# Stick-breaking exponents: a sum of the softplus of later key blocks, and one product with it per key block

## The reference, cut to what matters

```
z = q k^T * scale                                   # 512 queries x 512 keys, per head
causal = key < query
log_keep = where(causal, log_sigmoid(-z), 0)
suffix = reverse_cumsum_over_keys(log_keep) - log_keep
attn = where(causal, exp(log_sigmoid(z) + suffix), 0)
out = attn v
```

## Time and profile before

| | |
|---|---|
| median of 3 runs | 2204.77 us (2204.25 to 2207.14) |
| the profiled execution | 2204.68 us, its span 2202.9 us |
| PE busy | 2169.7 us, 98% of the span |
| DVE busy | 1253.3 us, 57% |
| ACT busy | 773.4 us, 35% |
| POOL busy | 25.7 us, 1% |
| HBM | 212.06 MB read, 98 GB/s over the span |

### The profile page before, as it was taken

One profiled execution on the slowest core, in us unless ns is written; L12 is line 12 of the kernel. 1 busy time (PEld: TensorE's weight loads), 2 busy tenths in 40 slices (PEclk: granted clock), 3 DMA queues, 4 the chain that ended last, 5 costly groups with the idle time before them and its releaser, 6 DMA issues.

```text
span 2202.9 us, 25712 instructions
## 1 busy us (share of the span) xinstructions
PE 2169.7 (98%) x10775; PEld 1804.6 (82%) x10775; DVE 1253.3 (57%) x1611; ACT 773.4 (35%) x1022; POOL 25.7 (1%) x42
## 2 busy tenths in 40 slices
PE   6999999999999899999999999999999999999998
PEld 3888888888888788987888888889898788888887
DVE  5898797953663847433855554234743475555422
ACT  2323232223353245344343333135434434333321
POOL 1000000000000000000000000000000000000000
PEclk9999999999999999999999999999999999999999
DMA  8432322333223122322223222322232222222322
GB/s 294 141 105 90 115 82 96 100 111 99 95 90 125 60 96 77 116 77 73 87 73 113 96 96 96 105 67 96 77 116 77 77 96 77 96 96 97 106 94 77
DMA packets 184151, 217.92 MB, mean 99 GB/s; under 512 B 3804, under 2 KB 159076, under 8 KB 184036
## 3 DMA queue, kind: packets, MB, share of 16 engines
q1 hardware_dynamic: 180048, 210.52, 28.8%
q10 hardware_dynamic: 3252, 3.60, 0.5%
q0 software_dynamic: 736, 2.15, 0.3%
HBM read 212.06 MB, written 4.19 MB: 98 GB/s over the span
## 4 chain that ended last, share of the span: by engine, by line
PE 94%; DVE 3%; ACT 1%; issue 1%; DMA 1%; POOL 0%; SPq 0%; POOLq 0%; ACTq 0%; DVEq 0%
PE psum L1640 30%; PE psum L1641 29%; PE psum L1642 29%; PE psum L1914 1%; PE psum L1945 1%; PE psum L1748 1%; PE psum L1977 1%; PE psum L1957 1%; DVE whl L475 1%; DMA ada<-in_w_ada 1%; DVE hT L1342 0%; PE psum L1901 0%; PE psum L1930 0%; POOL stat L620 0%; ACT hT L808 0%
## 5 line engine op out<-in xcount | busy, mean ns | idle before, releaser
L1640 PE MATMUL psum<-hT,whl 128*128 128x512 f32 (+1 forms) x2112 | 802.7, 380 | 7.7 <-DVE hT L1342 5.5
L1642 PE MATMUL psum<-hT,whl 128*128 128x512 f32 (+1 forms) x2112 | 795.9, 377 | 0.0
L1641 PE MATMUL psum<-hT,whl 128*128 128x512 f32 (+1 forms) x2112 | 795.9, 377 | 0.0
L475 DVE TENSOR_TENSOR whl<-raw,whl 128x1024 fp32r<-128x1024 f32 (+1 forms) x368 | 446.9, 1216 | 456.4 <-ACT whl L468 456.3
L468 ACT ACTIVATE whl<-raw 128x1024 fp32r<-128x1024 f32 (+1 forms) x368 | 384.2, 1047 | 445.6 <-PE psum L1642 430.8
L1640 PEld LDWEIGHTS psum<-hT,whl 128*128 128x128 f32 x2112 | 398.4, 189 | 89.0 <-issue 11.3
L1642 PEld LDWEIGHTS psum<-hT,whl 128*128 128x128 f32 x2112 | 398.3, 189 | 73.0
L1641 PEld LDWEIGHTS psum<-hT,whl 128*128 128x128 f32 x2112 | 398.6, 189 | 71.5 <-issue 0.5
L1640 PE MATMUL psum<-whl,ff 128*128 128x512 f32 x352 | 137.1, 389 | 0.0
L1642 PE MATMUL psum<-whl,ff 128*128 128x512 f32 x352 | 136.9, 389 | 0.0
L1641 PE MATMUL psum<-whl,ff 128*128 128x512 f32 x352 | 136.9, 389 | 0.0
(11 more groups left out here) (278 smaller groups left out, 2146.2 us busy)
## 6 DMA issues: line engine op xcount, KB each, us to landing
raw<-in_w_in SPq DMA_DIRECT2D x88, 1024.0 KB, 5.1
raw<-in_w_up SPq DMA_DIRECT2D x44, 1024.0 KB, 5.1
raw<-in_w_down SPq DMA_DIRECT2D x20, 1024.0 KB, 5.0
ada<-in_w_ada SPq DMA_DIRECT2D x12, 1024.0 KB, 14.3
raw<-in_w_branch SPq DMA_DIRECT2D x12, 1024.0 KB, 5.1
raw<-in_w_out SPq DMA_DIRECT2D x12, 1024.0 KB, 5.1
x<-in_x SPq DMA_DIRECT2D x4, 512.0 KB, 7.3
v_by_token<-vnat ACTq DMA_DIRECT2D x4, 512.0 KB, 2.9
```

What stands on the lines that cost most here:

```text
L475: nc.vector.tensor_tensor(whl_view(w, 1), raw_view(w), whl_view(w, 0).bitcast(F), ALU.subtract).then_inc(w_lo, 1)
L1640: M(out_, stat_hi, mov_hi, start=start, stop=False, **kw)
L1641: M(out_, stat_hi, mov_lo, start=False, stop=False, **kw)
L1642: return M(out_, stat_lo, mov_hi, start=False, stop=stop, **kw)
```

## The change

The softplus of the later key blocks is summed on DVE. `sbt` (640 columns) holds, for key block 0, the sum of the blocks 1 to 3 (384 columns), and for key block 1 the sum of the blocks 2 and 3 (256 columns); for key block 2 the only later block is block 3 itself. ACT makes the fp32r part of `sbt` and DVE its low part, and PE multiplies `negones_r` with these once per key block and part. That leaves (2+2) + (2+2) + (2+2) + 2 = 14 fp32r matmuls and 4 bfloat16 ones per head. The buffers lie in the memory of `sba`, the exponentials of the same pair, which ACT writes later; so DVE waits, for heads 2 and 3, until PE has read `sba` of the pair before (`sbo_ps`).

```diff
+    sbt = [over(f"sbt{e}", (sb_at[e] + 10) * K + 2560, [P, 640]) for e in range(2)]
+    sbt_hi = [over(f"sbt_hi{e}", (sb_at[e] + 10) * K, [P, 640], R) for e in range(2)]
+    sbt_lo = [over(f"sbt_lo{e}", (sb_at[e] + 10) * K + 2560, [P, 640], R) for e in range(2)]
...
                 def sb_hi(h):
                     act.wait_ge(sp_ready, 2 * (4 * l + h) + 2)
                     A(sphi[h % 2][:], sbs[h % 2][:], ACT.Copy).then_inc(sp_hi, 1)
+                    act.wait_ge(sp_sum, 4 * l + h + 1)
+                    A(sbt_hi[h % 2][:], sbt[h % 2][:], ACT.Copy).then_inc(sp_hi, 1)
...
+                    dve.wait_ge(sp_ready, 2 * (4 * l + h) + 2)
+                    if h >= 2:
+                        dve.wait_ge(sbo_ps, 2 * l + h // 2)
+                    step(V.tensor_copy(sbt[e][:, 384:512], sbs[e][:, 1024:1152]))
+                    later = step(V.tensor_tensor(sbt[e][:, 512:640], sbs[e][:, 1152:1280], sbs[e][:, 896:1024], ALU.add))
+                    step(V.tensor_copy(sbt[e][:, 0:128], sbs[e][:, 512:640]))
+                    dve.wait_ge(dve_chain, later)
+                    V.tensor_tensor(sbt[e][:, 128:384], sbs[e][:, 640:896], sbt[e][:, 384:640], ALU.add).then_inc(sp_sum, 1)
 
                 def sb_lo(h):
                     e = h % 2
-                    dve.wait_ge(sp_hi, 4 * l + h + 1)
-                    V.tensor_tensor(splo[e][:], sbs[e][:], sphi[e][:].bitcast(F), ALU.subtract).then_inc(sp_lo, 1)
+                    dve.wait_ge(sp_hi, 2 * (4 * l + h) + 2)
+                    step(V.tensor_tensor(splo[e][:], sbs[e][:], sphi[e][:].bitcast(F), ALU.subtract))
+                    V.tensor_tensor(sbt_lo[e][:], sbt[e][:], sbt_hi[e][:].bitcast(F), ALU.subtract).then_inc(sp_lo, 1)
...
                     for kb in range(TB):
                         c0 = Z_BANK[e] * SEQ + SBO[kb]
-                        for jb in range(kb, TB):
-                            for part in (sphi[e], splo[e]):
-                                M(psum[:, c0 + (jb - kb) * P:c0 + SBW[kb]], (negtri_r if jb == kb else negones_r)[:],
-                                  part[:, SBO[jb]:SBO[jb] + SBW[jb]], start=False, stop=False, skip_group_check=True)
+                        w_ = SBW[kb]
+                        for part in (sphi[e], splo[e]):
+                            M(psum[:, c0:c0 + w_], negtri_r[:], part[:, SBO[kb]:SBO[kb] + w_], start=False, stop=False, skip_group_check=True)
+                        for part, tail in ((sphi[e], sbt_hi[e]), (splo[e], sbt_lo[e])):
+                            if kb < 3:
+                                later = (tail[:, 0:384], tail[:, 384:640], part[:, SBO[3]:SBO[3] + P])[kb]
+                                M(psum[:, c0 + P:c0 + w_], negones_r[:], later, start=False, stop=False, skip_group_check=True)
                         ins = M(psum[:, c0:c0 + P], identb[:], sbaddb[:], start=False, stop=True, skip_group_check=True)
```

More of the change, by code:

```diff
@@ L388, in build @@
         hc_sum, sq_sum = sem("hc_summed"), sem("squares_summed")
-        rope_done, z_ps, sb_l, sp_ready, e_ps, sb_attn, sbo_ps, ob_hi, ob_lo = (
-            sem(n) for n in ("rope_done", "z_psum", "sb_log", "sp_ready", "e_psum", "sb_attn",
+        rope_done, z_ps, sb_l, sp_ready, sp_sum, e_ps, sb_attn, sbo_ps, ob_hi, ob_lo = (
+            sem(n) for n in ("rope_done", "z_psum", "sb_log", "sp_ready", "sp_summed", "e_psum", "sb_attn",
                              "sbo_psum", "ob_hi", "ob_lo"))
```

## The result

The changed kernel took 2215.86 us (median of 4, 2213.99 to 2217.05) against 2204.53 us (median of 4): 1.0048 times the time before, 95% interval 1.0031 to 1.0065. A second group of runs gave 1.0046 (1.0033 to 1.0058). The forecast was 2208.5 us in a range of 2206.6 to 2211.8, with 0.37 on slower by over 0.2% and 0.58 on no change within 0.2%. The direction of the sum was right; about 7 us of the loss were not in it, and the time lies above the range.

The account below looks back on a forecast made before the run. PE was taken to bound the kernel, busy 2169.7 of 2202.9 us. Waits of 7.28 us plus 0.40 us for restarts less 3.84 us saved gave +3.8 us on 2204.68: 2208.5 us, range 2206.6 to 2211.8.

Parts of the forecast that it names:

- PE's saving: In PE's exponents, six of 24 matmuls a head go: 0.48 us a head, 3.84 us in all, bounds 3.6 and 3.9.
- DVE's lateness: On DVE in front of head 1's `splo`, everything queued comes 3.13 us later per pair.
- the four waits for `sbt_lo`: PE waits for DVE's low part before head 1 in each of four pairs, 7.28 us over two layers.
- the surcharge of 0.05 us: On PE, the last fp32r matmul before the bfloat16 product takes 0.05 us extra, which moves to the new last one.
- DVE's additions: On DVE, waits, copies and adds lengthen `sb_softplus` by 0.96 us (0.83 to 1.18) and `sb_lo` by 0.74 us.
- the gap that took up 0.27 us: DVE's queue is idle 0.27 us in front of softplus 1, which takes up some of the added work.
- The wait: PE pauses before head 1 because DVE is late: 1.65 us in pair 0 and 1.99 us in pair 1.
- Head 0 doesn't wait: Head 0's `sp_lo`, 2.39 us later, comes at 838.84 and PE wants it at 840.81: no wait.
- Starting again: PE's first matmul after each wait costs 0.1 us extra, 0.4 us in all; bounds 0.05 and 0.27 us each.
- The rival of the clock: PE's clock halves for some 3 us of work behind each of four pauses, adding 6 us: 2214.5 us; 4%.
- The rival of small instructions that don't overlap: Each added DVE instruction ends before the next starts: 1.4 us more a pair on PE's wait, 2214.3 us; 6%.

Follow-up runs that it names:

- PE's part alone: The kernel before with PE's new loop of 14 fp32r products a head, reading `sphi` and `splo` in place of the sums, which are not made: 0.9979.
- filled: The changed kernel with seven products of 512 columns that nobody reads in front of PE's wait for the odd head: 1.0014.
- longer pause: The changed kernel with two more chained maxima of 256 columns on DVE in the softplus of the odd heads: 1.0060.
- one product: The changed kernel with one product of 512 columns that nobody reads in front of PE's wait for the odd head: 1.0020.
- DVE's part alone: The changed kernel with PE's old loop of 20 fp32r products a head; the sums and their two parts are still made: 1.0031.
- three products: The changed kernel with three products of 512 columns that nobody reads in front of PE's wait for the odd head: 1.0016.

## Why the prediction was wrong, point by point

The step that put the time above the range is the clock: the sum has no term for it, and the three falls that came cost 4.5 us in the pairs alone. The rest of the mechanism, PE's saving, DVE's lateness and the four waits for `sbt_lo`, came in kind as forecast, with these sizes:

- **PE's saving**, forecast 0.48 us a head: 0.59 us in the run of PE's part alone. The mis-sized term is the surcharge of 0.05 us in front of the bfloat16 product, which I let move to the matmul that is last then. It doesn't: in front of it a product of 384 columns takes 0.18 us (843.18 to 843.36 in PE's timeline after), as in mid-stream, and one of 256 columns 0.12 us. The surcharge showed only at 128-column products. The saving was 0.9 us larger by this, beyond my bound of 3.9 us. The half of it that is head 0's comes back as a longer wait, so the sum was 0.4 us too high by it.
- **DVE's additions**: 0.93 us for 0.96 in the softplus, 0.72 us for 0.74 in `sb_lo` (845.82 to 846.54, the start of the next split). Spacings from neighbouring rows, not durations, were right to 0.03 us, and so was the gap that took up 0.27 us.
- **The wait**: forecast 1.65 and 1.99 us of lateness, measured 846.67 - 844.94 = 1.73 us in pair 0 and some 2.1 us in pair 1, the difference being in the main the larger saving. Head 0 doesn't wait, as forecast. Starting again costs what was taken: filled or not, a pair is 6.65 to 7.0 us at full clock, 3.1 us above the kernel before in all, for +3.8 us forecast.
- **The rival of the clock** got 4% and was the case. Its price for a fall, 1.5 us, was right (2.15 - 0.58 = 1.6 us in pair 0). The failed step is the evidence against it: I took the granted clock behind one pause, of 0.80 us by the profile's count, and the pauses I forecast became 1.5 and 1.9 us by the same count. The trace before had a better witness, the 4.7 us wait in the earlier trace rows, whose clock I did not look up. PE waits there until 770.73, and the windows of the kernel before show the clock behind it:

```profile
766.00:772.00 6.00, 1.31 (x7) 0.85 0.00 0
772.00:774.00 2.00, 2.00 (x12) 0.59 0.02 3
```

The fall there begins during the wait, as some of the later ones did. A second witness in the trace before needs no wait at all. In both layers PE multiplies eight products of four rows for 2.06 us; in layer 1 the clock falls some 1 us behind them and costs about as much as behind a pause:

```profile
1767.16 2.12 PE L2005 MATMUL psum<-shares,sel_r 4*128 4x512 f32 x8
...
1770.40:1773.70 3.30, 3.30 (x10) 0.50 0.00 0
```

With the clock priced at four falls the sum would have been 2204.68 + 3.8 + 6 = 2214.5 us, as that rival's line said, 1.4 us below what was measured. That it comes so near is in part luck: three falls came and not four, and the gap was made up outside the pairs.
- **The rival of small instructions that don't overlap** was wrong. The added copy lasts 0.23 us and the next instruction starts after 0.14 us. The sentence of the Trainium skill, VectorE: DVE Perf Modes, "The DRAIN you can't avoid", that the next one can't start before the pipe is empty, does not hold for these instructions; its addition that a next one which is not held starts earlier agrees with this trace.

## What to carry to other kernels

On an engine that is busy 98% of the time, the price of a new wait is its length and also what the clock does behind it: look up the granted clock behind every wait of at least the forecast length in the trace at hand, and behind stretches of small products too. An edit that moves work from the bound engine to one that is 57% busy must be read against that engine's queue in front of the consumer, not against its share; here a saving of 4.7 us became a loss of 10 us, and two instructions per head moved ahead in that queue gave the 4.7 us back. Filling a wait with useless work on the waiting engine is a cheap test that separates lateness from what idleness brings.

## What the runs showed of the hardware

- TensorE's clock went from 2.4 to 1.2 GHz behind short pauses in an otherwise full stream. Of 14 profiled pauses of 1.5 to 2.8 us (changed kernel twice, longer pause, one product) 10 came with a fall, during the pause or up to 1.3 us behind it; of 10 pauses of 0.8 to 1.3 us (DVE's part alone, three products, one product) none did, nor did the waits of 1.32 and 0.80 us at 783 and 788 us in the profile before. Each fall behind a pause of 1.5 to 1.9 us in the changed kernel's profile cost about 1.5 us. Which ones fell was the same in three profiles (all but pair 0 of layer 1), and a pause of 2.4 us there did not bring one. Why is open. An idle PE isn't needed for a fall either: the kernel before has one behind 2.06 us of products of four rows (at 1770 us).
- On what sets the clock the Trainium skill, TensorE: Matmul & The Clock Gate, "The HAM clock gate", has a block that sets the clock by how busy PE was of late; that the clock stays up when the pause is filled with useless products agrees with it.
- A copy of 128 float32 columns on DVE is 0.14 us from start to start, and an add of 128 columns 0.20 us (827.06 to 827.26).
- The mean granted clock differs between executions of the same kernel (0.993 to 0.996 for the kernel before), in part by a stretch of half clock at the launch's start whose length varies; the kernel before took 2204.2 to 2208.6 us with it. One profile's span is then not to be compared with another's to within 5 us: the time from a pair's first matmul to the next tile was the measure that repeated to 0.03 us where the clock was full.
